# A ten-sub-block transformer on one core: the residual stream kept by tokens instead of by channels

## The reference, cut to what matters

```
x = x + 0.5 * (1 + gate) * rms_norm(swiglu(modulate(x, ...)), post_g)     # block 1: FFN, mixer, FFN
x = x + 0.5 * rmsnorm(swiglu(rmsnorm(x, pre_g)), post_g)                  # block 2: FFN, mixer, FFN
x = x + mixer(rmsnorm(x, g));  x = x + swiglu(rmsnorm(x, g))              # block 3: twice
return rmsnorm(x, g_final)
```

## Time and profile before

| | |
|---|---|
| median of 3 runs | 3627.2 us |
| profiled execution, its own span | 3626.8 us |
| TensorE busy | 96% |
| TensorE weight loads busy | 75% |
| VectorE busy | 54% |
| ScalarE busy | 31% |
| GpSimd busy | 4% |
| DMA | 325.75 MB, mean 90 GB/s |

### The profile page before, as it was taken

How to read it: one execution, slowest core, us unless ns; L and a number is a source line. 1 busy time by engine, 2 the same in 40 slices (tenths; PEclk the granted TensorE clock), 3 DMA queues, 4 the chain that set the end, 5 groups by cost and what they waited for, 6 DMA issues and landing times. The chain is left out here.

```text
span 3626.8 us, 45721 instructions
## 1 busy us (share of the span) xinstructions
PE 3478.4 (96%) x18518; PEld 2717.8 (75%) x18518; DVE 1965.9 (54%) x2658; ACT 1124.9 (31%) x1482; POOL 153.6 (4%) x127
## 2 busy tenths in 40 slices
PE   9999999999999999998799999999999999999998
PEld 7887776688878887677578886666788866568886
DVE  6667545622344333988553435795534358953334
ACT  2222334422232223342332223335322233542222
POOL 0000000000000000000000000330000022200000
PEclk7999999999999999999899999999999999999999
DMA  6554231122222222210022222210222221112221
GB/s 244 185 183 172 81 108 40 55 104 93 93 81 94 103 93 102 75 65 4 13 82 93 99 98 78 74 70 24 89 96 93 98 88 70 47 47 93 99 98 70
DMA packets 47231, 325.75 MB, mean 90 GB/s; under 512 B 5232, under 2 KB 5488, under 8 KB 8688
## 3 DMA queue, kind: packets, MB, share of 16 engines
q1 hardware_dynamic: 41792, 290.10, 22.4%
q0 software_dynamic: 5296, 33.61, 2.6%
HBM read 321.59 MB, written 2.10 MB: 89 GB/s over the span
## 5 line engine op out<-in xcount | busy, mean ns | idle before, releaser
L2107 PE MATMUL PS<-HH,WH 128*128 128x512 f32 x2264 | 895.5, 396 | 21.5 <-DVE HL L2531 15.9
L2108 PE MATMUL PS<-HL,WH 128*128 128x512 f32 x2264 | 884.1, 391 | 0.0
L2109 PE MATMUL PS<-HH,WL 128*128 128x512 f32 x2264 | 884.1, 391 | 0.0
L2513 DVE TENSOR_TENSOR WL<-RAW,WH 128x2048 fp32r<-128x2048 f32 x264 | 613.6, 2324 | 497.8 <-ACT WH L2366 497.5
L2366 ACT ACTIVATE WH<-RAW 128x2048 fp32r<-128x2048 f32 x264 | 503.0, 1905 | 297.4 <-PE PS L2109 289.5
L2107 PEld LDWEIGHTS PS<-HH,WH 128*128 128x128 f32 x2264 | 426.6, 188 | 140.3 <-issue 33.7
L2109 PEld LDWEIGHTS PS<-HH,WL 128*128 128x128 f32 x2264 | 426.6, 188 | 90.2
L2108 PEld LDWEIGHTS PS<-HL,WH 128*128 128x128 f32 x2264 | 427.0, 189 | 87.6 <-issue 1.4
L2107 PE MATMUL PS<-AH,WH 128*128 128x512 f32 x1056 | 412.5, 391 | 3.3 <-DVE A L2579 3.0
L2108 PE MATMUL PS<-AL,WH 128*128 128x512 f32 x1056 | 411.7, 390 | 0.0
L2109 PE MATMUL PS<-AH,WL 128*128 128x512 f32 x1056 | 411.5, 390 | 0.0
(11 more groups left out here) (412 smaller groups left out, 3596.7 us busy)
## 6 DMA issues: line engine op xcount, KB each, us to landing
RAW<-in_w SPq DMA_DIRECT2D x264, 1024.0 KB, 4.8
E<-in_ada POOLq DMA_DIRECT2D x28, 1024.0 KB, 5.1
E<-in_ada SPq DMA_DIRECT2D x4, 1024.0 KB, 12.0
G<-in_ada SPq DMA_DIRECT2D x4, 1024.0 KB, 20.3
X<-in_x SPq DMA_DIRECT2D x1, 2048.0 KB, 14.1
out_x<-A SPq DMA_DIRECT2D x8, 256.0 KB, 2.1
G<-in_cos POOLq DMA_DIRECT2D x4, 256.0 KB, 3.4
G<-in_sin POOLq DMA_DIRECT2D x4, 256.0 KB, 3.6
```

The lines of the kernel that those rows point to most:

```text
L2107: nc.tensor.matmul(out, wh, xh, start=start, stop=False)
L2108: nc.tensor.matmul(out, wh, xl, start=False, stop=False)
L2109: return nc.tensor.matmul(out, wl, xh, start=False, stop=stop)
L2513: nc.vector.tensor_tensor(WL[:, w % 2, :], RAW[:, w % 2, :], WH[:, w % 2, :].bitcast(F32), ALU.subtract).then_inc(w_lo, 1)
```

## The change

The residual stream is kept token-major: `XT` is four blocks of 128 tokens (partitions) by 1024 channels, in the memory of `X`; the input is loaded a second time as rows of tokens (`xn`), and the result is stored as four blocks of tokens.

- The last product of each sub-block is turned round: the activations (`AH`, `HH`) stand as TensorE's weights, the weight units as its moving operand with 512 output channels (`part`). A token block i fills the banks `PS[2i]` and `PS[2i+1]`. The last two units of a sub-block are walked together by token blocks (`leave`): block 0, 1, 2, 3 end one after the other. `out_projection` contracts by pairs of k, over all outputs of a token block, and waits with `freed` for its banks.
- A norm over channels is now a sum along a partition: ScalarE squares with an accumulated sum, and the root is a column of 128x1, with Ln and Exp on ScalarE and Newton on VectorE. The ones-products of the boundary and `keep_clock` are gone.
- Rows scaled by their root (`HG`, VectorE) are turned by eight transposes of 128x128 for each token block (`turn_tokens`, L2215), and high and low parts are made from PSUM for 256 tokens at a time (`hi`, `lo`).
- `enter` multiplies the next two units in two halves of 256 tokens each (where mix1 follows, one and a half units' worth: 72 matmuls in place of 96 before halving). Turns of blocks 2 and 3 stand inside the second unit's first half.
- Post gains become rows: for f10, m1, f11 `gain_rows` makes them by eight small products and ScalarE copies them (`gains`); the others are loaded by GpSimd's queue (`pool_gains`).
- Deferred FFNs and their scalings on VectorE are gone. The third unit's split stands behind `gains` where a sub-block has computed gains.
- The ada products of the boundary f10 to m1 stand between the halves of `enter`; those in the first down unit stand ahead of the last of four token blocks in place of the seventh of eight channel blocks.
- In mix2 VectorE takes variance 3 ahead of outputs 0 to 3 and the low blocks 4 to 7 (the convolution half) behind output 1. Banks are renamed by `PM = PS[4:] + PS[:4]`.

The core of the diff:

```diff
+            def part(src, w, i, tokens, begins, ends):
+
+                wh, wl = (x[:, w % 2, :].rearrange("p (k c) -> p k c", k=2) for x in (WH, WL))
+                for c in range(2):
+                    for n, (xh, xl) in enumerate(src):
+                        last = mm3(PS[2 * i + c][:], xh[:, tokens], xl[:, tokens], wh[:, n, c * S:(c + 1) * S],
+                                   wl[:, n, c * S:(c + 1) * S], begins and n == 0, ends and n == 1)
+                    if ends and 2 * i + c < 2 * NT - 1:
+                        last.then_inc(out_done, 1)
+                return last
+
+            def leave(s, w, first, second, second_arrives):
+
+                post, onward = plan["subs"][s]["post"], s + 1 < len(plan["subs"])
+
+                def one(u, i):
+                    return part((first, second)[u], w + u, i, slice(i * P, (i + 1) * P), False, u == 1)
+                one(0, 3)
+                one(0, 0)
+                second_arrives()
+                one(1, 0)
+                one(0, 1)
+                one(1, 1)
+                one(0, 2).then_inc(w_used, 1)
+                one(1, 2)
+                if onward:
+                    block_used(1, post)
+                    turn_tokens(0)
+                one(1, 3).then_inc(w_used, 1)
+                if onward:
+                    turn_tokens(1)
+
+            def enter(s):
+
+                w, (xh, xl), post = t("w"), halves(s), plan["subs"][s - 1]["post"]
+                units = [[(0, PS[4])], [(0, PS[5]), (1, PS[6])]] if plan["subs"][s]["kind"] == "mix1" else \
+                    [[(0, PS[4]), (1, PS[5])], [(0, PS[6]), (1, PS[7])]]
+                for half in range(2):
+                    cols_ = slice(256 * half, 256 * half + 256)
+                    for n, banks in enumerate(units):
+                        if half == 0:
+                            unit_arrives(w + n)
+                            block_used(2 + n, post)
+                        wh, wl = blocks(w + n)
+                        for k in range(KD):
+                            if n == 0:
+                                pe.wait_ge(hl_done, t("hl") + KD * half + k + 1)
+                            for c, bank in banks:
+                                last = mm3(bank[:, cols_], wh[:, KD * c + k, :], wl[:, KD * c + k, :],
+                                           xh[:, k, cols_], xl[:, k, cols_], k == 0, k == KD - 1)
+                            if half == 0 and n == 1 and k in (4, 6):
+                                turn_tokens(k // 2)
+                        if half:
+                            last.then_inc(w_used, 1)
+                    if half == 0 and s == 1:
+                        for a in range(ADA - ADA_SLOTS, ADA):
+                            ada(a, bank=TAIL_BANK, base=2 * (ADA - ADA_SLOTS))
+                t.add("hl", 2 * KD)
+                t.add("xs", NT)
+                t.add("hg", 2 * NT)
+                t.add("sqh", 2 * NT if post else 0)
+                if s in MADE:
+                    gain_rows(s, (PS[1], PS[2]) if plan["subs"][s]["kind"] == "mix1" else (PS[0], PS[1]))
...
+            def turn_tokens(i):
+
+                pe.wait_ge(xs_done, t("xs") + i + 1)
+                for k in range(KD):
+                    last = nc.tensor.transpose(turned_block(k, i % 2 * P, P), HG[:, i, k * P:(k + 1) * P], IDENT)
+                last.then_inc(turned, 1)
...
+            def gain_rows(s, banks):
+
+                at = CV_POST[s]
+                for k in range(KD):
+                    last = nc.tensor.matmul(banks[k // 4][:, k % 4 * P:k % 4 * P + P], CV[:, at + k:at + k + 1].to_broadcast([P, P]),
+                                            IDENT, start=True, stop=True)
+                    if k % 4 == 3:
+                        last.then_inc(gains_made, 1)
...
-            def keep_clock(n):
-
-                for _ in range(n):
-                    nc.tensor.matmul(PS[4 + (t("norms") + 1) % 2][:], ONES[:], CN[:, 0:S], start=True, stop=True)
...
+            def gains(s):
+
+                for c, to in enumerate(GAINS[s]):
+                    act.wait_ge(gains_made, 2 * MADE.index(s) + c + 1)
+                    src = (PS[1 + c] if plan["subs"][s]["kind"] == "mix1" else PS[c])
+                    nc.scalar.activation(to, src[:], ACT.Copy).then_inc(gains_ready, 1)
+
...
+                if post:
+                    square_out(0)
+                    root_out(0)
+                square_in(0)
+                if post:
+                    square_out(1)
+                    root_out(1)
+                square_in(1)
+                if onward:
+                    split(last_w)
+                if post:
+                    square_out(2)
+                    root_out(2)
+                if not onward:
+                    square_in(2)
+                    square_in(3)
+                else:
+                    if not post:
+                        square_in(2)
+                    hi(0)
+                    hi(1)
+                    if post:
+                        square_out(3)
+                        root_out(3)
+                    for n in range(2, 6):
+                        hi(n)
+                    split(last_w + 1)
+                    hi(6)
+                    hi(7)
+                    if post:
+                        square_in(2)
+                    square_in(3)
+                    for n in range(KD, 2 * KD):
+                        hi(n)
...
+                def gained(i):
+                    if i == 0:
+                        gains_arrive(dve, s)
+                    for c in range(2):
+                        dve.wait_ge(sqh_done, t("sqh") + 2 * i + c + 1)
+                        nc.vector.scalar_tensor_tensor(HG[:, i, c * S:(c + 1) * S], PS[2 * i + c][:], factor, GAINS[s][c],
+                                                       ALU.mult, ALU.mult).then_inc(hg_done, 1)
...
+                    dve.wait_ge(root_begun, t.add("roots"))
+                    chain(nc.vector.scalar_tensor_tensor(stat(i, 4), stat(i, 0), 1.0 / D, stat(i, 2), ALU.mult, ALU.add))
+                    i_[0] = i
+                    root = newton(stat(i, 4), stat(i, 3))
+                    if s == 0 and i == 0:
+                        dve.wait_ge(xn_loaded, 16)
+                    dve.wait_ge(hg_done, t("hg") + 2 * i + 2)
+                    nc.vector.scalar_tensor_tensor(XT[:, i, :], HG[:, i, :], root, XT[:, i, :], ALU.mult, ALU.add).then_inc(x_done, 1)
...
+                def normed(i):
+                    dve.wait_ge(sqx_done, t("sqx") + i + 1)
+                    chain(nc.vector.tensor_scalar(stat(i, 10), stat(i, 8), 1.0 / D, EPS, ALU.mult, ALU.add))
+                    dve.wait_ge(root_begun, t.add("roots"))
+                    i_[0] = i
+                    root = newton(stat(i, 10), stat(i, 9))
+                    dve.wait_ge(x_done, t("x") + i + 1)
+                    if onward:
+                        nc.vector.tensor_scalar(HG[:, i, :], XT[:, i, :], root, None, ALU.mult).then_inc(xs_done, 1)
...
+                for i in (0, 1):
+                    if post:
+                        gained(i)
+                    add_out(i)
+                    normed(i)
+                if post:
+                    gained(2)
                 else:
-                    ins.then_inc(sq_added, 1)
+                    add_out(2)
+                if not onward:
+                    add_out(3)
+                    normed(2)
+                    normed(3)
+                else:
+                    split(last_w)
+                    if post:
+                        add_out(2)
+                    for n in range(2):
+                        lo(n)
+                    if post:
+                        gained(3)
+                    else:
+                        add_out(3)
+                    for n in range(2, 6):
+                        lo(n)
+                    if post:
+                        add_out(3)
+                    split(last_w + 1)
+                    lo(6)
+                    lo(7)
+                    normed(2)
+                    normed(3)
+                    for n in range(KD, 2 * KD):
+                        lo(n)
...
             root("a")
+            variance(3, "b", 0)
             out(0, "a", 0)
             out(1, "a", 1)
-            variance(3, "b", 0)
+            dve.wait_ge(silu2, 4)
+            for m in range(4, KD):
+                lo(m)
             out(2, "a", 2)
             root("b")
             out(3, "b", 0)
             for m in range(4):
-                dve.wait_ge(silu2, m + 1)
-            for m in K_ORDER["mix2"]:
                 lo(m)
 
+        def pool_gains(pool, s):
+
...
-                def scale(u, i=0):
-                    dve.wait_ge(w_used, w + u + 1 + i)
-                    nc.vector.tensor_tensor(V[:], PS[2 * (u % 2)][:], R[:], ALU.mult).then_inc(gate_scaled, 1)
-                    if u:
-                        dve.wait_ge(act_ready, base + u + i)
```

(30 more changed lines are left out.)

711 lines of the change are left out of this document (336 added, 375 removed).

## The result

The changed kernel takes 3656.97 us (median of 4 runs, 3655.73 to 3657.78), the kernel before 3626.95: a ratio of 1.0085, 95% interval 1.0071 to 1.0100. It is 30 us slower where 18.5 us less were forecast, and outside the range of 3580 to 3645. The profiled execution has a span of 3655.3 us, 28.5 more than before.

The account below looks back on a forecast made before the run. TensorE, busy 96% of the span, was taken as the bound. Gains elsewhere of 19.0 us less 0.5 lost at the boundaries gave 18.5 us off the 3627.2 us median: 3609 us, range 3580 to 3645.

Parts of the forecast that it names:

- the change leaves their work as it is: Steady stream: products of 512 columns stay as they are, 0.2267 us each; only what lies between them can move.
- weight loads of half products: Rival: 256-column products are bound by their weight loads, 0.16 to 0.22 us each; 3659 us at 0.16; chance 0.13.
- the low clock: Rival: the 3.8 us waits also lower TensorE's clock, 4 us at each of nine boundaries, 3645 us; chance 0.12.
- Boundaries: The nine boundaries between sub-blocks together bring nothing: 167.5 us of extra against 167.0 before.
- the transposes: At each boundary, 32 transposes of two records each, 0.110 us a record: 7.0 us.
- two long waits: Behind the boundaries into m1 and f11, TensorE waits for the third unit's weights; 2.6 us of low clock added each.
- Half products: At the boundaries, products of 256 columns start every 0.120 us, so halving costs 1.3 us a boundary.
- Tail: From the last product to the span's end: 8.9 us instead of 15.4, 6.5 gained.
- Mix2's output: The convolution half enters first, TensorE starts 4.8 us earlier and is spared a few waits: 5.1 us gained.
- Sub-block 1: First down unit: the ada products' wait nearly goes, the clock stays up, gain rows add 1.8 us: 6.5 us gained.
- Mix1's output: Two sums move behind two token blocks: 0.9 us gained.
- VectorE's scalings in four FFNs: Two extra scalings per unit go, but they lie beside products and bring nothing.

Follow-up runs that it names:

- a1: The changed kernel with its spacer LINE 32 columns wider, so that the buffers behind it lie where they lay in the kernel before: 3594.5 us.
- d4: As a1, with VectorE's order at mix2's output put back as in the kernel before: 3600.95 us.
- c1: As a1, with ScalarE's copies of the gain rows moved behind the third unit's split in f11 and m1: 3585.29 us.
- a2: The changed kernel with its spacer LINE 16 columns wider: 3643.15 us.

## Why the prediction was wrong, step by step

**The step that failed** is in the first part: "the change leaves their work as it is". I priced every product of 512 columns by the trace of before, 0.2267 us, and looked only at what lies between them. 0.2333 came in its place (a1 against after: 62 us). The cue stood in the diff: four entries of `PV` went, and the buffer is allocated ahead of the operands; beside it a spacer `LINE`, 8 columns wide and used by nothing, fills the sum of the widths up to a round number. No rival had this mechanism; the slower side's rivals were weight loads of half products and the low clock.

With the buffers in place the change is 30.7 us faster than the runs of before beside it (35.3 by the two profiled spans), where 18.5 was forecast: the sign was right, the size was not. By its terms, a1 against before:

- **Boundaries**: forecast 0.5 lost (167.5 against 167.0 in its windows of 40 us), measured 13.6 gained by the table. The step mis-sized is that of the transposes: I read two records for each out of the earlier trace rows and took 7.0 us a boundary. It is one record (eight for a turn, 32 a boundary and not 64, 0.109 apart in the rows of a1 above), so 3.5 us. Where no post norm stands in the way this comes off in full: 8.3, 9.2 and 8.3 for 11.8. With a post norm, TensorE is through with its turns 1.7 us earlier, and waits so much longer for the first low half, 5.27 for 3.8, which VectorE sets; 14.4 to 16.8 stand for 16.3 and 17.3. Into m1 and f11 it is 37.0 and 32.4 for 35.7 and 30.2; the steps listed for their two long waits add up to 6.7 and 5.9, not the 6.5 and 5.7 that entered the sum, and 6.12 and 6.76 were measured.
- **The low clock**: as forecast. In a1 the 5.27 us wait into mix2 brings it down; the granted clock is the number behind TensorE's busy time:

```profile
1460.00:1464.00 4.00, 4.00 (x20) 0.51 0.49 176
1464.00:1468.00 4.00, 2.69 (x22) 1.00 0.00 0
```

  It is 0.51 of full speed, the lower level, in the 4 us behind the wait, and full again from 1464. Twenty half products start 0.213 us apart in place of 0.120. But behind them TensorE waits for the seventh low half anyway (1.31 us), so little is lost, and the rival that put 4 us on each boundary falls. The two waits for weights, into m1 and f11, had 2.6 each in the forecast and show 0.50 too, from 480 to 484 and from 739 to 743.
- **Half products**: forecast 0.120 us. In a1 0.1196, after 0.1183; the rows of the changed kernel, 24 halves apart:

```profile
1507.79 0.28 PE L2136 MATMUL PS<-HH,WH 128*128 128x256 f32 x1
...
1510.63 0.28 PE L2136 MATMUL PS<-HH,WH 128*128 128x256 f32 x1
```

The rival of weight loads falls: its 0.135 is not reached.

- **Tail**: forecast 6.5 gained, measured 6.9.
- **Mix2's output**: forecast 5.1, measured 5.4, and shown by d4.
- **Sub-block 1**: forecast 6.5, measured 0.3 in a1 and 1.9 in c1. The ada products' wait went from 6.16 to 0.72, as forecast; the gain rows cost a wait of 2.7 that was not in the sum and take 3.1 (in c1 2.0) in place of 1.8. The forecast also had the clock stay up, but right behind the ada products it is still at the lower level for 3.4 us (317 to 321 in a1, 319 to 323 in c1), which at half speed costs 1.7. For c1 these terms give 6.5 - 2.7 - 0.2 - 1.7 = 1.9, as measured, and for a1 0.8.
- **Mix1's output**: forecast 0.9, measured 0.1.
- **VectorE's scalings in four FFNs**: forecast nothing, measured 1.0 each. Before, one gap of 0.9 us stood at the first down unit of each (in f20 from 1328.9); it is gone.
- **The start**: TensorE's first product came at 50.7 before and at 47.2 in a1, but at 50.5 after and 51.0 in c1: 3.6 of the 35.3 us between the two spans are this scatter. The terms add up to 34.0; 1.1 more lie in the first 96 products.

## What to carry to other kernels

Before a diff's instructions are priced, price its memory map: list the buffers in their order with their widths before and after, and ask which operands of the commonest instruction moved against each other. In a profile, read the spacing of the steady stream first and compare it with that of before; if it differs where the code is unchanged, no step of the diff explains it. A regression may hold a gain: here a spacer of 128 bytes turned 30 us slower into 31 us faster, and only then the queue orders were worth tuning.

## What the runs showed of the hardware

- A product of 512 columns (fp32r, the type of the high and low parts) started every 226.7 ns when its two operands lay a multiple of 256 bytes apart in a partition, every 232.4 or 233.3 ns when they lay 128 off it, and every 233.3 or 228.9 ns at 64 off it, depending on which operand is loaded. That is up to 2.9%. VectorE's split of 128x2048 took 2.32 us in both kernels, ScalarE's 1.91, and no group of eight or more of their instructions differs by as much as 1 us in all between after and a1: the place of the buffers shows on TensorE.
- Products of 256 columns at full clock were not slower with the operands off, but a little faster: they started on average every 0.1196 us in a1, 0.1187 in after (128 off) and 0.1148 in a2 (64 off).
- A transpose of 128x128 left one record and started 0.109 us behind the one before, where a plain float32 product of 128 columns left two (the eight of L2206 are x16 above). The reading of two for both, in the table's notes ahead of the prediction, was wrong for transposes.
